# Attention rebuilt with keys on partitions, the sums of its weights added on GpSimd alone

## What is computed

```python
def attend(qb, k, v):
    s = jnp.einsum("bhgqd,bhkd->bhgqk", qb, k).astype(jnp.float32) * (HEAD_DIM ** -0.5)
    p = jax.nn.softmax(s, axis=-1).astype(v.dtype)
    return jnp.einsum("bhgqk,bhkd->bhgqd", p, v)

def gqa_branch(q_l, k_l, v_l, q_c, k_c, v_c, q_g, k_g, cos, sin, need_ctx):
    ql = apply_rope(rms_norm_2(to_heads(q_l, ATT_HEADS), q_g), cos, sin)
    kl = apply_rope(rms_norm_2(to_heads(k_l, ATT_KV_HEADS), k_g), cos, sin)
    kc = rms_norm_2(to_heads(k_c, ATT_KV_HEADS), k_g)
    k_all = jnp.concatenate([kl, kc], axis=2)
    v_all = jnp.concatenate([vl, vc], axis=2)
    ...
```

## Time and profile before

| what | value |
|---|---|
| three executions | 6234.52, 6248.83, 6249.45 us; median 6248.83 us |
| profiled execution | 6240.71 us; its span from first to last instruction 6238.9 us |
| mean granted TensorE clock | 0.927 of full speed |
| TensorE busy | 5562.8 us, 89% of the span |
| VectorE, ScalarE, GpSimd busy | 2588.9, 1832.2 and 415.8 us |

### The profile page before, as it was taken

The page is one execution under the profiler, slowest core; times in us unless marked ns, Lnnn a source line. Parts: engine busy times, 40 slices in busy tenths (PEclk is TensorE's granted clock), DMA queues, the critical chain, the costliest instruction groups (busy, mean ns, idle before and its releaser), DMA issues. The chain is left out here.

```text
span 6238.9 us, 77765 instructions
## 1 busy us (share of the span) xinstructions
PE 5562.8 (89%) x30564; PEld 4117.8 (66%) x30564; DVE 2588.9 (41%) x5898; ACT 1832.2 (29%) x4322; POOL 415.8 (7%) x661
## 2 busy tenths in 40 slices
PE   4979998998996989699999988969987999999889
PEld 2338886785556766567777467757655677775667
DVE  2220124443334456625555036344656255551354
ACT  2221004441114311124444123133111144442231
POOL 0000010000000011210000000010222200000000
PEclk8999998866777999999999999989998999999999
DMA  4001101105422000000000110330000000001112
GB/s 162 14 14 45 44 7 76 54 34 190 136 82 85 14 8 1 18 7 1 1 1 1 42 59 9 120 108 21 1 8 11 14 1 1 1 1 42 59 54 95
DMA packets 145405, 256.16 MB, mean 41 GB/s; under 512 B 10796, under 2 KB 89748, under 8 KB 144404
## 3 DMA queue, kind: packets, MB, share of 16 engines
q1 hardware_dynamic: 107700, 211.32, 9.7%
q10 hardware_dynamic: 37344, 39.85, 1.9%
HBM read 195.15 MB, written 55.98 MB: 40 GB/s over the span
## 5 line engine op out<-in xcount | busy, mean ns | idle before, releaser
L1973 PEld LDWEIGHTS ps_pv<-y_t,probs_t 128*128 128x128 f32 x4640 | 588.2, 192 | 153.3 <-issue 142.9
L2050 DVE TENSOR_REDUCE soft<-ps_scores 128x1 f32<-128x512 f32 (+1 forms) x648 | 410.3, 633 | 495.4 <-PE ps_scores L1936 494.1
L1973 PE MATMUL ps_pv<-y_t,probs_t 128*128 128x64 f32 x4640 | 579.4, 270 | 31.4 <-DVE y_t L2088 30.8
L1287 DVE TENSOR_TENSOR features_low<-h_t,features_high 128x1024 fp32r<-128x1024 f32 x260 | 304.0, 1171 | 354.9 <-ACT features_high L1252 354.4
L654 PE MATMUL ps_proj<-weight_ring,h_t 128*128 128x256 f32 x2048 | 448.5, 381 | 2.7 <-PE ps_proj L654 2.2
L654 PEld LDWEIGHTS ps_proj<-weight_ring,h_t 128*128 128x128 f32 x2048 | 388.8, 191 | 57.7 <-issue 5.4
L2029 ACT ACTIVATE probs<-ps_scores,soft 128x512 f32<-128x512 f32 (+1 forms) x648 | 408.0, 642 | 16.2 <-DVE soft L2059 16.2
L2015 ACT ACTIVATE probs_t<-ps_pt 128x512 f32<-128x512 f32 (+1 forms) x392 | 205.1, 523 | 685.3 <-PE ps_pt L1953 675.4
L1224 PE MATMUL ps_proj<-features_high,weights_high 128*128 128x512 f32 (+1 forms) x880 | 345.9, 393 | 59.6 <-DVE features_low L1287 30.3
L1252 ACT ACTIVATE features_high<-h_t 128x1024 fp32r<-128x1024 f32 x260 | 259.7, 1001 | 421.2 <-PE ps_proj L1224 359.2
L1953 PE MATMUL ps_pt<-ident,probs 128*128 128x128 f32 x2320 | 370.4, 278 | 7.7 <-ACT probs L2029 7.6
(11 more groups left out here) (307 smaller groups left out, 9120.4 us busy)
## 6 DMA issues: line engine op xcount, KB each, us to landing
weight_ring<-in_w_in_dram SPq DMA_DIRECT2D x40, 1024.0 KB, 5.3
mod_weights<-in_w_mod_dram ACTq DMA_DIRECT2D x24, 1024.0 KB, 5.2
x_rows<-h_rows SPq DMA_DIRECT2D x32, 512.0 KB, 5.7
t_rows<-t_rows SPq DMA_DIRECT2D x64, 256.0 KB, 2.6
x_res<-h_rows SPq DMA_DIRECT2D x32, 512.0 KB, 3.5
res<-result SPq DMA_DIRECT2D x48, 264.0 KB, 2.0
res_rows<-res SPq DMA_DIRECT2D x48, 264.0 KB, 3.9
h_t<-v_rows SPq DMA_DIRECT2D x3, 4096.0 KB, 13.8
```

The source lines that it names most:

```text
L1287: dve.tensor_tensor(self.fl[:, s % NB, :, 0:n], self.hT[:, k0:k0 + KS, c0:c0 + n], self.fh[:, s % NB, :, 0:n].bitcast(F32), ALU.subtract). ...
L1973: mm = pe.matmul(pv[:, 0:HD], pT[:, before(u, c) % 4, j * P:(j + 1) * P], VN[:, k0 + k, kv * HD:(kv + 1) * HD], start=(k == 0), stop=(k == ...
L2050: dve.tensor_reduce(st[:, u % 2, 0, c:c + 1], ps[c][:, 0:tiles(u, c) * P], AXX, ALU.max).then_inc(mx.h, 1)
```

## The change

`stage_attend` is written anew. Scores are made transposed, with 128 keys on partitions and 512 query columns (256 query rows by two heads) along the free axis, so that exp leaves the weights as the values' matmul wants them and no weight is transposed. Work goes by groups of 256 query rows (8, and in layer 0 a ninth for the context rows, of 2 key tiles) and by slots of one key tile (18 in a group): 146 slots in layer 0, 144 in layer 1. In a slot TensorE adds up in PSUM, for both key heads, a float32r matmul of 128 rows (q rounded to float32r against k's rounded and low half), one of 64 rows (q's low half against k's rounded half) and one of one row (ones times the negated maxima). Then it does one piece of the next group's maxima, a plain scores matmul with queries on partitions, which VectorE reduces. ScalarE's exp takes 128 x 1024. TensorE multiplies with the values in four float32 matmuls with 64 output partitions each. The sums over keys are kept in one 128 x 1024 buffer: with `LEAN = ()` GpSimd adds every slot's weights to it, in two instructions of 128 x 512, and VectorE none. When a group is done, TensorE sums that buffer over partitions (`total`), in the fourth slot of the next group, and GpSimd may write its first sum of the new group only then. The weights lie in three buffers, so exp of slot s waits for the sums of slot s-3 (of s-2, where s-3 is a group's first).

In `stage_qkv2` queries are no longer transposed; `stage_attend` does that (`turn_q`). A key tile is transposed twice, to either half of the partitions; ScalarE rounds it (`high`, four copies) and VectorE takes the rest (`low`, two subtractions), four units behind. The az projection moves to the head of the new `stage_attend`, in pairs of 64 output partitions, between the first group's maxima. `stage_output2` loads two of its eight weight tiles in two DMAs each, since the rows of the attention's output lie in another order.

```diff
-def stage_attend(env, QT, keys, VN, aT, qtiles):
+def stage_attend(env, hT, qR, KA, VN, aT, spare, with_ctx, zchunks):
...
+    LEAN = ()
...
             def scores(s):
...
+                if s >= 2:
+                    pe.wait_ge(ex.h, ex.at(s - 1))
...
+                for kv in range(2):
+                    pe.matmul(sT[b][:, kv, :], KA[:, kv, ks], flat(QA[:, g % 2, kv, :, :]), start=True, stop=False)
+                for kv in range(2):
+                    lo = slice(HD * kv, HD * (kv + 1))
+                    pe.matmul(sT[b][:, kv, :], KA[lo, kv, ks], flat(QB[lo, g % 2, :, :]), start=False, stop=False)
+                if j == 0:
+                    pe.wait_ge(mr.h, mr.at(2 * g + 2))
+                for kv in range(2):
+                    r = slice(HD * kv, HD * kv + 1)
+                    mm = pe.matmul(sT[b][:, kv, :], one[r, :], flat(MR[r, g % 2, :, :]), start=False, stop=True)
...
+            def values(s):
+                g, j = slots[s]
+                pe.wait_ge(ex.h, ex.at(s + 1))
...
+                for half in range(2):
+                    cs = slice(half * GT, (half + 1) * GT)
+                    for kv in range(2):
+                        lo = slice(HD * kv, HD * (kv + 1))
+                        mm = pe.matmul(pO[lo, cs], VN[:, groups[g][1] + j, lo], pT[s % 3][:, kv, cs],
...
+            for s, (g, j) in enumerate(slots):
+                if g + 1 < G and j < 2:
+                    turn_q(g + 1, j)
+                if g >= 1 and s == den_slot(g - 1):
+                    total(g - 1)
+                if g + 1 < G and j in (10, 17):
+                    turn_max(g + 1, j // 17)
+                if s + 1 < N:
+                    scores(s + 1)
+                for x in hosted(g, j)[0]:
+                    maxima(g + 1, x)
+                values(s)
+                for x in hosted(g, j)[1]:
+                    maxima(g + 1, x)
...
         @block.scalar
...
+            for s, (g, j) in enumerate(slots):
+                act.wait_ge(sm.h, sm.at(s + 1))
+                if s >= 3:
...
+                    act.wait_ge(pvm.h, pvm.at(s - 2))
+                    act.wait_ge(pa.h, pa.at(n_p))
...
+                act.activation(pT[s % 3], sT[s % 2][:, :, :], ACT.Exp, scale=HD ** -0.5).then_inc(ex.h, 1)
...
+        @block.gpsimd
...
+                pool.wait_ge(ex.h, ex.at(s + 1))
+                if j == 1 and g >= 1:
+                    pool.wait_ge(dn.h, dn.at(g))
+                for kv in range(2):
...
+                        ins = pool.tensor_tensor(acc[:, kv, :], acc[:, kv, :], pT[s % 3][:, kv, :], ALU.add)
+                    ins.then_inc(pa.h, 1)
```

and in `stage_qkv2`:

```diff
             def turn(u):
                 g, t, nh = units[u]
+                if g == 0:
+                    return
                 pe.wait_ge(st.h, st.at(u + 1))
...
+                if t >= 2:
+                    pe.wait_ge(kl.h, kl.at(t - 1))
...
+                if u >= 4:
+                    low(u - 4)
```

More of the change, by code:

```diff
@@ L1736, in _ @@
             sp.dma_start(gn[:, 1, :], A["k_norm_g_2"][layer:layer + 1, :].to_broadcast([P, HD])).then_inc(ld.h, 16)
[L1737 to L1741 removed]
+            env.load_groups(sp, g0 + 2 + 1)
         @block.tensor
@@ new lines, in stage_attend, with hosted @@
+    parts = [list(chunks(g)) for g in range(G)]
+    chunk0 = [sum(len(p) for p in parts[:g]) for g in range(G + 1)]
+    def hosted(g, j):
+        if g + 1 >= G:
+            return (), ()
+        n, nk = len(parts[g + 1]), groups[g][2]
+        at = [1 + x * (nk - 3) // n for x in range(n)]
+        here = [x for x in range(n) if at[x] == j]
+        return here[:1], here[1:]
+    sums = {}
+    n_pool = n_dve = 0
+    for s, (g, j) in enumerate(slots):
+        n_pool += (j >= 1) + (j >= 1 and j not in lean(g))
+        n_dve += j in lean(g)[1:]
+        sums[s] = (n_pool, n_dve)
@@ L2004, in _, with turn_q @@
-            rows(U - 1)
+            wz = env.group_here(pe, g0)
+            def turn_q(g, t):
+                tile = groups[g][0] // P + t
+                if t == 1:
+                    pe.wait_ge(ql.h, ql.at(2 * g + 1))
+                elif g >= 1:
+                    pe.wait_ge(mr.h, mr.at(2 * g))
+                for h in range(4):
+                    rows = qR[:, tile, h * HD:(h + 1) * HD]
+                    pe.transpose(px[0:HD, h * P:(h + 1) * P], rows, env.ident[:, :])
+                    mm = pe.matmul(px[HD:P, h * P:(h + 1) * P], rows, env.ident[:, :], start=True, stop=True)
+                mm.then_inc(qt.h, 1)
@@ new lines, in total @@
+            def total(g):
+                if g + 1 < G:
+                    pe.wait_ge(ql.h, ql.at(min(2 * g + 6, 2 * G)))
+                else:
+                    pe.wait_ge(rc.h, rc.at(g))
+                n_p, n_d = sums[first[g + 1] - 1]
+                pe.wait_ge(pa.h, pa.at(n_p))
+                if lean(g):
+                    pe.wait_ge(da.h, da.at(n_d))
+                for kv in range(2):
+                    two = kv == 1 and lean(g)
+                    mm = pe.matmul(px[HD * kv:HD * (kv + 1), :], env.ones[:, 0:HD], acc[:, kv, :], start=True, stop=not two)
+                    if two:
+                        mm = pe.matmul(px[HD * kv:HD * (kv + 1), :], env.ones[:, 0:HD], acc2, start=False, stop=True)
+                mm.then_inc(dn.h, 1)
```

567 lines of the change are left out of this document (314 added, 253 removed).

## The result

The changed kernel takes **6169.98 us** (median of four, 6164.76 to 6171.31) against 6249.14 for the kernel before on the same chip: ratio 0.9878, 95% interval 0.9862 to 0.9893. It is 79 us faster, not 279, and lies 10 us above the predicted range. The profiled execution has a span of 6167.3 us; mean granted clock 0.91, against 0.927.

What follows compares the result with a forecast made beforehand. TensorE was taken to bound the kernel (97% busy in az and attention). From 6240.7 us, 330 less for az and attention and 59 more for the projections gave 5970; overall range 5790 to 6160, the forecast's own 5900 to 6050.

Steps and rivals of the forecast that it cites:

- the wait for them: Attention, a group's fourth slot: TensorE waits 2.0 us for an exp held up by GpSimd's additions, which start after `total`.
- 59.8: Attention: us per group, from 56.1 of TensorE work plus 3.7 of waits, against 77.9 in the old kernel.
- The rival of GpSimd as the bound: Attention: shape changes are hidden and GpSimd's additions set a group at 49.0 us, 5802 in all; chance 0.13.
- the one of serial row halves: Attention: float32r matmuls in row halves run one after the other, 11.9 us more a group, 6156 in all; chance 0.13.
- Two `turn_q` add 1.7: Attention: turning a group's query rows costs TensorE 1.7 us, priced as eight matmuls of 128 columns in column halves.
- A brief fall after each wait: TensorE's clock falls briefly after its waits of 2.0 and 2.8 us, costing 30 us in all, within the range.
- holds one reduction up, 0.6: Attention, a group's seventh slot: VectorE's division delays one maxima reduction, adding 0.6 us to the group.
- A step of the rivals: Under stretched GpSimd additions: GpSimd contends only with VectorE instructions of two SBUF inputs, two a group, so nothing changes.
- Key units of 7.0 us: Projections, 12 key tiles a layer: 3.45 projection, 2.8 stall on VectorE's `low`, 0.77 for four matmuls in column halves.
- the two faster rivals: GpSimd as the bound (5802 us) and float32r row halves running serially (6156 us), chance 0.13 each.
- the slower side: Stretched GpSimd additions (6450 us), half clock (up to 6560) or no matmuls side by side (6514); chance 0.11 together.
- sum of small losses: Case in which small losses add up until no gain is left; chance 0.03.

Runs made afterwards that it cites:

- Experiment 4: Changed kernel with two identity matmuls instead of a transpose and a matmul for query rows, maxima and key rows: 6127.0 us, ratio 0.9815.
- Experiments 5 and 6: Changed kernel, TensorE adding zeros during its wait for GpSimd (5: 6135.11 us), or also during its wait for VectorE before the tenth maxima piece (6: 6129.09 us).
- experiment 8: Changed kernel with earlier `total`, later division end, four key banks, identity matmuls for transposes, and GpSimd additions cut to 8 columns outside each group's second slot: 5890.26 us.
- experiment 2: Changed kernel with the division's last reciprocal quarter and two multiplications moved two slots later, from a group's seventh to its ninth: 6118.58 us, ratio 0.9795.
- experiment 1: Changed kernel with `total` one slot earlier, in the second slot after the group's first instead of the third: 6099.95 us, ratio 0.977.

## Why the prediction was off

Right: the direction; the length of a slot (2.97 for 2.91), with row halves side by side and the shape changes paid; GpSimd's additions (1.29 us on average) beside TensorE's work; the wait for them, its place and its size; the key units' stall and its cause. With the long waits and the clock's falls taken away and the transposes made as priced, a group takes 59.5 us; that this is so near 59.8 is luck, for 2.0 of the 59.8 were the wait for GpSimd, which that kernel no longer has. The rival of GpSimd as the bound fell (43 of 71.7 us busy; 0.8 us a group for all its work), the one of serial row halves too, although its 6156 is nearly the time measured: the two starts of a pair in L2025 are 0.003 us apart.

Wrong, against the 199 us between the profiled execution, 6169.1, and 5970:

- **"Two `turn_q` add 1.7 (eight matmuls of 128 columns in column halves)".** The eight are four transposes and four matmuls. They were priced from the earlier trace rows, where both halves have matmuls. 34 calls x 1.52 = 52 us, `turn_max` 34 x 0.47 = 16 (1.02 each for 0.55), and 0.4 in each key unit. Experiment 4 shows it (0.97 us for a `turn_q`).
- **"A brief fall after each wait costs 1 to 2 us, 30 in all".** The fall was seen as a rival and as part of the range, and stood at zero in the sum. It cost 5.4 us in each of ten groups, 54, and 1.7 in every other key unit, 20. The only row of a fall stands behind 3.54 us of waiting, and nothing in the old attention waits that often; 2 us were taken to do next to nothing. Experiments 5 and 6 show it.
- **The division "holds one reduction up, 0.6".** It held it for 1.76 us at full clock (1.33 where the clock had fallen before), since two pieces of maxima, the reciprocal, two multiplications and the longer reduction stand in a row: 1.16 x 12 groups = 14 us, and a second idle time in the period. A step of the rivals failed here too: that GpSimd's contention touches two VectorE instructions a group is right, that "nothing changes" by it is not. The two are these multiplications. Without GpSimd beside them they take 1.39 us together (experiment 8), here 2.35, and 2.78 in layer 0's first group. Take the 0.96 and 1.39 us off the two waits and 0.37 is left of either, less than the 0.6 forecast: an estimate, as no run took the additions away from the changed kernel itself.
- **Key units of 7.0 us.** They took 7.7 at full clock, 24 x 0.7 = 17, of it the 0.4 above.
- 0.06 us more in 290 slots, 17.

That makes 52 + 16 + 74 + 14 + 17 + 17 = 190 of 199. The rest I have not split.

The range took in the two faster rivals, while the slower side was left at the mechanisms' sizes one by one. Four small losses that pull the same way, and the clock that multiplies two of them, were given 0.03 as a "sum of small losses".

## What to carry to other kernels

Price a wait on TensorE twice: for its idle time, and for what the clock does after it. In a loop whose period holds two waits of 1 to 2 us the second price can be larger than the first (5.4 us a group for falls, 3.2 for the waits); taking either wait away, or filling both with work on zeros, won most of it back.

A pair of instructions in two halves of the array is worth its price only if rows show that same pair; a transpose beside a matmul is not two matmuls. And an engine that is 40% busy can still hold up the others: what counts is how much of its work stands in one slot, and what runs beside it there. An addition on an engine with time to spare had its price on another, in the two instructions that TensorE's wait hung on.

## What the runs showed of the hardware

- The clock fell after waits of 1.89 and 1.33 us in one group, in ten groups, each time at the same two places (5.5 and 26.0 us after the start of `total`). It stayed at full through 1.89 and 1.76 us in the first group of each layer, and in eleven of twelve groups through 1.89 us alone in experiment 2; a lone wait of 1.76 us in experiment 5 brought it down in ten of twelve, a lone one of 1.33 us in experiment 1 in seven of twelve. What decides between these is open; no run here varied the place of a wait alone. The Trainium skill (TensorE: Matmul & The Clock Gate, A second HAM failure mode: psum-queue depth-cycling) tells of short idle times between groups of matmuls that make the clock swing; the trace agrees, with waits of 1.33 and 1.89 us.
- The records of float32 matmuls of 128 columns with the identity, in column halves, start in pairs 0.11 us apart, so that eight matmuls (16 records) take 0.97 us with the change of shape; four transposes and four matmuls take 2.37.
- A float32r matmul in row halves shares the array as float32 does: two of 512 columns, 0.43 us together with the change of shape.
- A VectorE multiplication of 128 x 512 with both operands in SBUF takes 0.69 us where GpSimd adds nothing beside it, up to 2.1 us where additions come in twos, and 23.20 us, once, where 18 follow in a row; a reduction of 128 x 1024 from PSUM takes 1.22 us in every case.
